# Two-layer hybrid backbone on one core: order of the start-up loads, later constants, and no copy of x in layer one

## What is computed

```python
def layer(x, mod, p):
    s1, sc1, g1, s2, sc2, g2 = split(silu(c) @ w_ada + b_ada, 6)
    h = layer_norm(x) * (1 + sc1) + s1
    hy, wq, wk, wv, rq, rk, rv, rg, cq, ckv, krope, gates = split(h @ w_in)
    y_a = hyena(hy)          # short conv, then two long convolutions with
                             # filters sin(sin(z w1 + b1) w2 + b2) w3 * decay
    y_b, y_c, y_d = window_attention, retention, latent_attention
    x = layer_norm(ALPHA * x + g1 * (merged @ w_out))
    h2 = layer_norm(x) * (1 + sc2) + s2
    return layer_norm(ALPHA * x + g2 * moe(h2))
```

## Time and profile before

| | |
|---|---|
| median of 3 runs | 1837.55 us (1827.86 to 1841.9) |
| the profiled execution | 1837.38 us, of which span 1835.7 us |
| instructions in the profile | 29410 |
| PE busy (matmul) | 1552.4 us, 85% of the span |
| PE weight loads | 1283.0 us, 70% |
| DVE busy | 901.6 us, 49% |
| ACT busy | 720.1 us, 39% |
| POOL busy | 188.0 us, 10% |
| mean granted TensorE clock | 0.908 of full speed |
| DMA | 273.34 MB, mean 149 GB/s |

### The profile page before, as it was taken

How to read it: one execution, slowest core, us unless ns; L and a number is a source line. 1 busy time by engine, 2 the same in 40 slices (tenths; PEclk the granted TensorE clock), 3 DMA queues, 4 the chain that set the end, 5 groups by cost and what they waited for, 6 DMA issues and landing times.

```text
span 1835.7 us, 29410 instructions
## 1 busy us (share of the span) xinstructions
PE 1552.4 (85%) x9368; PEld 1283.0 (70%) x9368; DVE 901.6 (49%) x1591; ACT 720.1 (39%) x1215; POOL 188.0 (10%) x224
## 2 busy tenths in 40 slices
PE   2899997989997589889769999898899957988884
PEld 1878896776886477667548888777768846766673
DVE  1654544333446543565737446334243465455756
ACT  2342425341233533455333533344312354344643
POOL 0001100000000352201000100000000004430010
PEclk9799897999999699999859999888999977999997
DMA  9322243442342236877172221434333503568740
GB/s 356 112 92 69 69 142 111 159 149 91 112 153 80 103 122 230 304 287 251 58 283 93 70 81 59 158 127 151 110 112 121 181 13 144 177 214 329 282 164 34
DMA packets 74442, 273.34 MB, mean 149 GB/s; under 512 B 9292, under 2 KB 9580, under 8 KB 72624
## 3 DMA queue, kind: packets, MB, share of 16 engines
q1 hardware_dynamic: 66384, 239.44, 37.7%
q0 software_dynamic: 7904, 31.98, 4.6%
HBM read 254.97 MB, written 17.76 MB: 149 GB/s over the span
## 4 chain that ended last, share of the span: by engine, by line
PE 57%; DVE 17%; DMA 9%; ACT 6%; issue 4%; DVEq 4%; ACTq 1%; SPq 1%; POOL 0%; POOLq 0%
PE psum L977 6%; PE psum L978 5%; PE psum L979 5%; PE psum L1353 4%; DMA ring<-units_ada 4%; DMA ring<-units_in 4%; PE psum L1533 3%; DVE ring_lo L2198 3%; PE psum L1474 2%; PE psum L1476 2%; PE psum L1475 2%; DVE ring_lo L2289 2%; PE psum L1512 2%; ACT w_hi L1747 2%; PE psum L1513 1%
## 5 line engine op out<-in xcount | busy, mean ns | idle before, releaser
L2289 DVE TENSOR_TENSOR ring_lo<-ring,u_hi 128x1024 fp32r<-128x1024 f32 x116 | 143.4, 1236 | 331.1 <-ACTq L1831 325.9
L977 PE MATMUL psum<-x_hi,u_hi 128*128 128x384 f32 x736 | 264.4, 359 | 23.0 <-DVEq L2291 14.1
L978 PE MATMUL psum<-x_lo,u_hi 128*128 128x384 f32 x736 | 254.5, 346 | 0.0
L979 PE MATMUL psum<-x_hi,ring_lo 128*128 128x384 f32 x736 | 254.2, 345 | 0.0
L1830 ACT ACTIVATE u_hi<-ring 128x1024 fp32r<-128x1024 f32 x116 | 122.7, 1058 | 269.6 <-DMA ring<-units_in 191.5
L977 PEld LDWEIGHTS psum<-x_hi,u_hi 128*128 128x128 f32 x736 | 145.1, 197 | 39.3 <-issue 16.0
L978 PEld LDWEIGHTS psum<-x_lo,u_hi 128*128 128x128 f32 x736 | 145.2, 197 | 1.6 <-issue 0.5
L979 PEld LDWEIGHTS psum<-x_hi,ring_lo 128*128 128x128 f32 x736 | 144.5, 196 | 0.0
L2198 DVE TENSOR_TENSOR ring_lo<-ring,w_hi 128x1024 fp32r<-128x1024 f32 x96 | 118.3, 1232 | 39.8 <-ACTq L1748 31.6
L1056 PE MATMUL psum<-ring,condS 128*32 128x128 f32 x1536 | 68.2, 319 | 60.9 <-DMA ring<-units_ada 60.9
L1747 ACT ACTIVATE w_hi<-ring 128x1024 fp32r<-128x1024 f32 x96 | 101.7, 1059 | 42.6 <-PE psum L1514 24.9
(11 more groups left out here) (411 smaller groups left out, 3212.6 us busy)
## 6 DMA issues: line engine op xcount, KB each, us to landing
ring<-units_moe SPq DMA_DIRECT2D x132, 512.0 KB, 5.3
ring<-units_in SPq DMA_DIRECT2D x116, 512.0 KB, 3.5
ring<-units_ada SPq DMA_DIRECT2D x96, 512.0 KB, 4.6
R<-units_moe SPq DMA_DIRECT2D x60, 512.0 KB, 6.6
ring<-units_br SPq DMA_DIRECT2D x32, 320.0 KB, 2.9
ring<-units_out SPq DMA_DIRECT2D x16, 512.0 KB, 3.5
expert_out_rows<-RE POOLq DMA_DIRECT2D x12, 512.0 KB, 6.8
x_of_layer<-X POOLq DMA_DIRECT2D x2, 1536.0 KB, 10.7
```

The lines of the kernel that those rows point to most:

```text
L977: mm(o, hi[:, c], x_hi[:, k, :], start=k == 0, stop=False)
L978: mm(o, hi[:, c], x_lo[:, k, :], start=False, stop=False)
L979: i = mm(o, lo[:, c], x_hi[:, k, :], start=False, stop=k == DT - 1)
L2289: V.tensor_tensor(ring_lo[:, slot_of(u), :], ring[:, slot_of(u), :, :].rearrange("p a b -> p (a b)"), u_hi[:, n % 2, :].bitcast(F32), ALU. ...
```

## The change

Four things are changed.

1. Loads. SP's head of queue is now condS (on a semaphore of its own, `cond_loaded`), the first 146 columns of the constants (ident, row_sel and expert_sel, which now lead CONSTS), and X; engines wait for `cst_ready` 32. ACT's Silu of the condition waits for the condition alone. Of the parameters only b_ada (48 columns, now first in PARTS) is loaded after ada1; the other 2608 columns are issued by SP after ada15, in both layers.
2. POOL waits until ada15 has landed, and then issues in layer one the other 4914 columns of constants, w3, hydec, dist, and the router arrays; in layer two w3, hydec, dist. DVE waits for the parameters and for these constants (`cst_rest_ready` 48) when it enters hy, PE at fil1, ACT at vT.
3. The copy of X to x_dram is left out in layer one; X comes back from x_in. In layer two POOL stores it, waits until it is stored, and then sets `x_free`, for which DVE waits before its first x_lo. For this POOL's program is written out for each layer in place of a loop.
4. fil1 stands behind hy, and fil2 behind rk.

```diff
 def stages():
...
          ("hT", [], [f"hT{d}" for d in range(DT)]),
-         ("fil1", [], ["fil1"]),
          ("hy", [f"hy{i}" for i in range(6)], [f"hy{i}" for i in range(6)]),
-         ("fil2", [], ["fil2"]),
+         ("fil1", [], ["fil1"]),
          ("rk", ["rk0", "rk1"], ["rk0", "rk1"]),
+         ("fil2", [], ["fil2"]),
          ("rq", ["rq0", "rq1"], ["rq0", "rq1"]),
...
         def _(sp):
-            sp.dma_start(cst[:], consts).then_inc(cst_ready, 16)
-            sp.dma_start(rw[:], router_w).then_inc(cst_ready, 16)
-            sp.dma_start(rb[:], router_b).then_inc(cst_ready, 16)
-            sp.dma_start(condS[:], cond).then_inc(cst_ready, 16)
+            sp.dma_start(condS[:], cond).then_inc(cond_loaded, 16)
+            sp.dma_start(cst[:, 0:FIRST_CONST], consts[:, 0:FIRST_CONST]).then_inc(cst_ready, 16)
             sp.dma_start(X[:], x_in).then_inc(cst_ready, 16)
...
+                    n = PART_AT["b_ada"][1]
                     if i == 1:
-                        sp.dma_start(prm[:], params[l]).then_inc(prm_ready, 16)
+                        sp.dma_start(prm[:, 0:n], params[l, :, 0:n]).then_inc(b_ada_ready, 16)
+                    if u == f"ada{ADA_UNITS * ADA_FIRST - 1}":
+                        sp.dma_start(prm[:, n:N_PARAM], params[l, :, n:N_PARAM]).then_inc(prm_ready, 16)
...
         def _(pool):
...
+            def one_layer(l):
...
                 pool.wait_ge(layer_free, l + 1)
                 settle(pool)
-                pool.dma_start(x_dram, X[:]).then_inc(x_stored, 16)
+                if l:
+                    pool.dma_start(x_dram, X[:]).then_inc(x_stored, 16)
+                    pool.wait_ge(x_stored, 16 * l)
+                pool.sem_inc(x_free, 1)
+                last = f"ada{ADA_UNITS * ADA_FIRST - 1}"
+                pool.wait_ge(slot_loaded[slot_of(last)], loading(l, last))
+                settle(pool)
+                if l == 0:
+                    pool.dma_start(cst[:, FIRST_CONST:N_CONST], consts[:, FIRST_CONST:N_CONST]).then_inc(cst_rest_ready, 16)
                 pool.dma_start(w3[0:HY_FFN, :], hy_w3[l]).then_inc(rows_ready, 16)
                 pool.dma_start(hydec, hy_decay).then_inc(rows_ready, 16)
                 pool.dma_start(dst, dist).then_inc(rows_ready, 16)
+                if l == 0:
+                    pool.dma_start(rw[:], router_w).then_inc(cst_rest_ready, 16)
+                    pool.dma_start(rb[:], router_b).then_inc(cst_rest_ready, 16)
...
-                pool.dma_start(X[:], x_dram).then_inc(x_loaded, 16)
+                pool.dma_start(X[:], x_in if l == 0 else x_dram).then_inc(x_loaded, 16)
...
         def _(act):
-            act.wait_ge(cst_ready, 80)
+            act.wait_ge(cond_loaded, 16)
             F(condS[:], condS[:], ACT.Silu).then_inc(cond_ready, 1)
+            act.wait_ge(cst_ready, 32)
...
                 elif name == "hy":
+                    dve.wait_ge(prm_ready, nth(l, prm_ready, 16))
+                    dve.wait_ge(cst_rest_ready, 48)
```

More of the change, by code:

```diff
@@ L116, in stages @@
          ("hT", [], [f"hT{d}" for d in range(DT)]),
+         ("hy", [f"hy{i}" for i in range(6)], [f"hy{i}" for i in range(6)]),
          ("fil1", [], ["fil1"]),
-         ("hy", [f"hy{i}" for i in range(6)], [f"hy{i}" for i in range(6)]),
+         ("rk", ["rk0", "rk1"], ["rk0", "rk1"]),
          ("fil2", [], ["fil2"]),
-         ("rk", ["rk0", "rk1"], ["rk0", "rk1"]),
          ("rq", ["rq0", "rq1"], ["rq0", "rq1"]),
@@ L729, in build @@
         x_split = sem("x_split", DT)
-        x_stored = sem("x_stored", 16)
+        x_stored = raw_sem("x_stored")
+        x_free = sem("x_free", 1)
         x_loaded = sem("x_loaded", 16)
@@ L1633, in store_rows @@
-            def store_rows(r, t):
-                i = HELD_AT[(r, t)]
-                _, row, n, at = TILES[r][t]
-                pool.wait_ge(out_dve, nth(l, out_dve, i + 1))
-                if r in SMALL:
-                    settle(pool)
-                    for h in range(2):
-                        pool.dma_start(out_rows_dram[at:at + n, h * 512:(h + 1) * 512],
-                                       out_rows[h * HALF + row:h * HALF + row + n, i % 2, 0:512]).then_inc(rows_out[i % 2], 16)
-                    return
-                pool.wait_ge(out_act, nth(l, out_act, sum(q not in SMALL for q, _ in HELD_TILES[:i + 1])))
-                settle(pool)
-                pool.dma_start(out_rows_dram[at:at + n, :], out_rows[row:row + n, i % 2, :]).then_inc(rows_out[i % 2], 16)
@@ L1648, in _ @@
-            for d in range(DT):
-                pool.wait_ge(x_hi_ready, nth(l, x_hi_ready, DT + d + 1))
-                settle(pool)
-                nc.gpsimd.tensor_tensor(h_lo[:, d, :], h2[:, d, :], h_hi[:, d, :].bitcast(F32), ALU.subtract)
-                pool.drain()
-                pool.sem_inc(h_split, 1)
-            pool.wait_ge(slots_ready, nth(l, slots_ready, 1))
-            build_one_hot(GATHER_ORDER[1])
-            for step in STEPS:
-                if step[0] == "ga" and step[3] == DT and GATHER_ORDER.index(step[1]) + 2 < len(CHUNKS):
-                    build_one_hot(GATHER_ORDER[GATHER_ORDER.index(step[1]) + 2])
-                elif step[0] == "dn" and step[1] not in DENSE:
-                    for t in range(len(TILES[step[1]])):
-                        store_rows(step[1], t)
@@ L1677, in _ @@
-            layer.close()
+                    nc.gpsimd.tensor_tensor(h_lo[:, d, :], h2[:, d, :], h_hi[:, d, :].bitcast(F32), ALU.subtract)
+                    pool.drain()
+                    pool.sem_inc(h_split, 1)
+                pool.wait_ge(slots_ready, nth(l, slots_ready, 1))
+                build_one_hot(GATHER_ORDER[1])
+                for step in STEPS:
+                    if step[0] == "ga" and step[3] == DT and GATHER_ORDER.index(step[1]) + 2 < len(CHUNKS):
+                        build_one_hot(GATHER_ORDER[GATHER_ORDER.index(step[1]) + 2])
+                    elif step[0] == "dn" and step[1] not in DENSE:
+                        for t in range(len(TILES[step[1]])):
+                            store_rows(step[1], t)
@@ new lines, in one_layer @@
+                job = step_jobs(("gu", ORDER[-3], 0))[-1]
+                pool.wait_ge(filled[bank(job)], filling(l, job))
+                settle(pool)
+                pool.dma_start(lnr2, ln_rows[l, :, 2:4, :]).then_inc(ln2_ready, 16)
+                for i in range(2):
+                    pool.wait_ge(rows_out[i], nth(l, rows_out[i], per_layer[rows_out[i].name]))
+                pool.wait_ge(weights_ready, nth(l, weights_ready, 1))
+                settle(pool)
+                for t in range(NT):
+                    for x in range(2):
+                        n = x * NT + t
+                        pool.indirect_dma_start(
+                            out=back_rows[:, x, t, :], out_offset=None, in_=out_rows_dram,
+                            in_offset=bass.IndirectOffsetOnAxis(ap=slot_i[:, n:n + 1], axis=0),
+                            bounds_check=N_SLOT - 1, oob_is_err=False).then_inc(rows_back[t], 16)
@@ L1680, in _ @@
+            pool.wait_ge(cst_ready, 32)
+            for l in range(DEPTH):
+                one_layer(l)
         @block.scalar
```

179 lines of the change are left out of this document (92 added, 87 removed).

## The result

The changed kernel took 1817.78 us (median of 4 runs, 1814.46 to 1820.26), the kernel before 1839.18 us in the same comparison: ratio 0.9882 [0.9847, 0.9917], 21.4 us less. Measured a second time, beside more runs of the kernel before, it was 1814.29 against 1840.34 us: 0.9858 [0.9842, 0.9875], 26.0 us less. Both intervals are clear of 1: the kernel is 1.2 to 1.4% faster. The forecast was 1809.4, or 28.1 us less than the 1837.5 it started from.

A forecast was written before the change was run, and what follows sets the result against it. The prediction took PE's chain as the bound, with each layer's start waiting for modulation units behind bytes queued ahead of ada15. Its terms summed as 1837.4 - 17 - 7 - 4 = 1809.4 us, range 1798 to 1825.

The forecast's parts named there:

- A: Rival, layer one: POOL's late constants run slower than 168 GB/s and DVE's new wait decides; 1816 us, chance 0.12.
- B: Rival: start of layer two gains nothing, the copy of X and ScalarE's idle hold ada15; 1815 to 1816 us, chance 0.10.
- C: Rival: the moved sine chains expose PE at fil1 and fil3, +1.7 us in place of -4; 1815 us, chance 0.08.
- Term 1: Start of layer one: fewer bytes ahead of X and ada15, so ada15 ends at 33.6 instead of 51.06; -17 us.
- 0.5 us for hy0 and hy1: Layer one: parameters push hy0 and hy1 back 3.5 us, nearly covered by ScalarE and DVE work; 0.5 us charged.
- The late constants: Layer one: POOL's 4.10 MB after ada15 land at some 51 us, pessimistically 57.9, in time for hy2; nothing charged.
- The even half: Layer one after ada15: queues taking turns give POOL's constants half of 380 GB/s, landing at 55 us; sum unchanged.
- 3.2 us for a unit: Start of layer one: by this transfer rule four slots would not hold PE back; ada15 near 29, sum 1805 us.
- Term 2: Start of layer two: parameters and POOL's tables leave the ada stretch, shortening PE's waits; -7 us, bounds -1 and -9.9.
- Term 3: Filter's two sine chains, each layer: moved later, they shorten PE's ring_lo waits; 2.0 us per layer, -4 us.
- D: Rival, whole run: TensorE's granted clock falls from 0.908; at 0.885 it costs 40 us, 1849 us, chance 0.04.
- E: Rival, start of layer one: the ring runs at PE's rate; 1805 us, chance counted within the forecast's 0.66.

The follow-up runs named there:

- the late store: Changed kernel with POOL's store of X in layer two behind ada15 and the late parameters behind hy1; 1806.53 us, measured again 1805.13 us.
- the part alone: Kernel before with only fil1 moved behind hy and fil2 behind rk; 1837.10 us against 1840.34, ratio 0.9972.

## Why the prediction was right, point by point

- **The number.** 21.4 and 26.0 us were gained where 28.1 were forecast. By time alone, 1817.78 and 1814.29 us lie nearer to the 1815 to 1816 of rivals A, B and C than to 1809.4; what speaks for the forecast are the marks.
- **What bounds the start** held: the chain there is unit landings before and after, DMA share 0.93 against 0.95.
- **Term 1, -17; measured -15.6 at ada15, -15.4 at the first hy.** The ring's rate held: from ada3 to ada15 I had 12/8 x 13.46 = 20.2 us, measured 34.37 - 14.07 = 20.30. That it fits to a tenth is luck, for the seven profiles with this head have 18.7 to 20.5. What failed is the step before it, "X lands at 7.1": it landed at 8.8, with the first group at 10.20 (8.5 predicted) and ada3 at 14.07 (12.3). What was mis-sized is the term of 7.6 us: taking 2.66 MB out brought X's landing from 14.7 to 8.8, 5.9 us, which is 450 GB/s. I had priced these bytes at 348 GB/s, the mean of a stretch with its slow start in it; but the slow start stays (the slices of the changed kernel begin at 0, 3, 218 and 198 GB/s before they reach 355), and the bytes that went had run at the rate of the slices behind it, mostly over 400. This is nearly all of the miss. With the mean of the seven profiles, 34.3, the gain at ada15 is 16.3 us.
- **0.5 us for hy0 and hy1**: the cover is as said in four of six profiles, and too small in two (0.9 and 4.3 us). I had weighed the parameters alone; the step left out that POOL's transfers run beside hy1's unit.
- **The late constants** were charged at nothing, and cost nothing. They landed at 54.7; expected some 51, pessimistically 57.9. Their rate was 4.10 MB in 19.8 us, 207 GB/s. They cost nothing by 2 us: VectorE's last x_lo ended at 56.7.
- **The even half, and 3.2 us for a unit.** The Trainium skill ("DMA: Bandwidth & Descriptors", Queues, rings and completion order) has each DMA engine take turns between queues, a packet at a time. My even half of 380 GB/s, an estimate from that rule, gave 55. The landing at 54.7 agrees with it, but by luck: the transfers began 1.4 us later than I had them, and the two queues did not share evenly. From 37 to 49 us POOL's queue (q0) and SP's (q1) moved, in MB:

```profile
q0 software_dynamic: 253, 2.97, 64.2%
q1 hardware_dynamic: 462, 1.67, 37.7%
```

  In the kernel before, from 17 to 33 us, it was 3.01 MB each. So SP's units got about a third of the bytes while hy1 and hy2 were under way. The other rule, 3.2 us for a unit, is stated by the same page (Anatomy of one DMA) for transfers that GpSimd issues; these units are issued by SyncE, up to four at a time, and the chain's pieces are 5.13 to 5.72 us. X, 1536 KB with only the condition and 73 KB of constants ahead of it, took 7.1 us.
- **Term 2, -7; measured -6.2** from the first group to ada15, -6.7 counted from SP's first unit (911.49 before, 895.80 after). The sixteen units of six profiles with this head take 29.2 to 30.6 us where the kernel before took 35.4, so -6.2 is the best of them and -5.6 their mean. The 3.83 us did not go entirely: of them 1.35 stayed at ada2, now for VectorE, and 1.54 came up at ada1. The bound of -9.9 is about what the late store reaches: +25.9 and +26.2 against +35.4 is 9.2 to 9.6 less.
- **Term 3, -4; measured -3.2** with the part alone, and -2.2 and -3.7 from ada15 to fil3 in the changed kernel's two profiles. The mechanism is as said; two sizes were off. The two waits left 0.5 us (the sum took all 2.8, though the signs beside it said 0.5), and the wait for x_lo grew by 1.0 where I charged 0.8 for fil1.
- **Sum.** The terms as measured are 15.6 + 6.2 + 2.2 = 24.0, against 28 forecast, and the two comparisons gave 21.4 and 26.0. Between the two profiles compared here the unchanged stretches took back 0.7 us in layer one and 5.8 in layer two, which leaves about the 17.6 of the last mark.
- **Signs.** X at 8.8 (7 to 8 said), the first group at 10.2 (8.5) and ada15's start at 34.4 (31 to 34) are all a little late, by the one term above. Ada15 of layer two, 6.7 us sooner (7), and 0.5 us for ring_lo came as said, and none of the signs of being wrong appeared.
- **Rivals.** A (late constants decide): no, but nearer than thought, and with part 4 undone it is what happens (7.6 us at PE). B (layer two gives nothing): no; but its mechanism, the store of X, does hold 3 us. C (sine chains expose PE): no. D (the granted clock): no; the mean clock went from 0.908 to 0.911 and not down. But PE busy grew by 8.7 us with the same matmuls at that slightly higher mean, so the 17 us per hundredth of the mean do not describe it, and the unchanged stretch spreads by 7.4 us in layer one and 11.3 in layer two. It does not turn the result, but it is as large as any error above. E (ring at PE's rate): no; PE waited for units until the end.

## What to carry to other kernels

Where a start waits for the last of many queued units, count the bytes in front of that unit and not the time of the first matmul: starting PE 4.1 us sooner gained nothing, and moving transfers behind ada15 did (shown in layer one for each of the three, in layer two for the store of X and the tables). Then look at what stands behind the moved transfer on its own queue, and which engine takes that in order ahead of the critical work: the parameters in front of hy0 are harmless in one execution and cost 4 us in the next, and two units further back they cost nothing in three profiles. For edits worth less than the spread of the times, compare marks in the trace from one dependence to the next, and take each mark from several executions: one and the same head put ada15 at 32.9 in one and at 35.0 in another.

## What was not expected of the hardware

- A transfer put back into the head of layer one, whose DMA engines are 0.90 to 0.93 busy, cost 2.4 to 4.1 us against the mean of seven profiles, where its bytes at the head's rate are 4.2 to 4.9 us.
- One 512 KB unit took 15.2 us to land with 1304 KB ahead of it on its queue and 4.1 MB on POOL's, and the same program had it 3 to 5 us sooner in two other executions. In such a stretch the two queues moved 2.97 and 1.67 MB, where they had moved 3.01 MB each in the kernel before.
- The unchanged stretch of some 800 us differs by up to 11.3 us between profiles, together with the time at the low clock level. Which executions get how much of it stays open: the kernels without the change lie in the middle, those with it at both ends.
